# One ring of eight raw slots in the first stage, evenly spread modulation units, and high parts made straight from the slab

## The reference

```python
def ada_params(cond, w, b):
    mod = jax.nn.silu(cond) @ w + b
    return jnp.split(mod, 3, axis=-1)
...
sh_l, sc_l, g_l = ada_params(c, ada_w[layer], ada_b[layer])
sh_c, sc_c, g_c = ada_params(c_ctx, ada_w[layer], ada_b[layer])
xm_l = x_lat * (1.0 + sc_l) + sh_l
xm_c = x_ctx * (1.0 + sc_c) + sh_c
...
mem_n = rmsnorm(mem, norm_mem_w[l])
k = (mem_n @ w_k)
```

## Time and profile before

| | |
|---|---|
| three runs | 3175.62, 3176.96 and 3183.54 us; median 3176.96 us |
| the profiled execution | 3178.01 us |
| its span, first to last instruction | 3176.2 us |
| mean granted TensorE clock | 0.991 of full speed |
| PE busy | 97% of the span |
| DVE busy | 71% |
| ACT busy | 51% |
| data moved | 666.42 MB, mean 210 GB/s |

### The profile page before, as it was taken

How to read it: one execution, slowest core, us unless ns; L and a number is a source line. 1 busy time by engine, 2 the same in 40 slices (tenths; PEclk the granted TensorE clock), 3 DMA queues, 4 the chain that set the end, 5 groups by cost and what they waited for, 6 DMA issues and landing times.

```text
span 3176.2 us, 45015 instructions
## 1 busy us (share of the span) xinstructions
PE 3093.1 (97%) x16842; PEld 2658.5 (84%) x16842; DVE 2244.8 (71%) x2732; ACT 1633.4 (51%) x1984; POOL 59.5 (2%) x52
## 2 busy tenths in 40 slices
PE   7999999999999999999999999999999999999998
PEld 5787877888788887888888888888888888888887
DVE  6779987788768787655767865567457777777544
ACT  6655444555534566544456655445345555555443
POOL 0002300000000000000000000000000000000000
PEclk8999999999999999999999999999999999999999
DMA  7977784787568664655555555566445555555554
GB/s 293 339 256 270 255 296 172 264 311 239 181 211 289 244 220 159 208 182 183 176 186 175 168 189 194 190 225 198 142 146 181 190 189 188 185 185 196 188 191 139
DMA packets 180248, 666.42 MB, mean 210 GB/s; under 512 B 20084, under 2 KB 20468, under 8 KB 178808
## 3 DMA queue, kind: packets, MB, share of 16 engines
q1 hardware_dynamic: 178424, 660.09, 61.2%
q10 hardware_dynamic: 1664, 4.19, 0.3%
HBM read 657.91 MB, written 6.29 MB: 209 GB/s over the span
## 4 chain that ended last, share of the span: by engine, by line
PE 82%; DVE 10%; DMA 3%; ACT 2%; DVEq 1%; issue 1%; ACTq 0%; SPq 0%
PE acc L760 44%; PE acc L764 22%; DVE w_lo L1980 4%; PE acc L771 3%; PE acc L773 3%; PE acc L772 3%; DMA ada_raw<-in_w_ada 1%; ACT w_hi L1275 1%; DVE mod_raw L1991 1%; DMA mod_raw<-in_w_mod 1%; PE acc L928 1%; PE msc L1170 0%; DMA raw<-in_w_mix_out 0%; PE msc L874 0%; PE msc L1190 0%
## 5 line engine op out<-in xcount | busy, mean ns | idle before, releaser
L1980 DVE TENSOR_TENSOR w_lo<-raw,w_hi 128x1024 fp32r<-128x1024 f32 x1020 | 1242.3, 1228 | 561.2 <-ACT w_hi L1275 551.8
L1275 ACT CAST w_hi<-raw 128x1024 fp32r<-128x1024 f32 x1020 | 1061.8, 1049 | 803.2 <-PE acc L764 556.9
L760 PE MATMUL acc<-a_pair,w_hi 128*128 128x512 f32 x2944 | 931.8, 398 | 9.8 <-DVE w_lo L1980 4.1
L764 PEld LDWEIGHTS acc<-a_pair,w_lo 128*128 128x128 f32 x2944 | 554.0, 188 | 131.0
L764 PE MATMUL acc<-a_pair,w_lo 128*128 128x256 f32 x2944 | 579.3, 278 | 0.0
L760 PE MATMUL acc<-b_pair,w_hi 128*128 128x512 f32 x1792 | 571.0, 400 | 5.9 <-DVE w_lo L1980 5.9
L760 PEld LDWEIGHTS acc<-a_pair,w_hi 128*128 128x128 f32 x2944 | 451.2, 189 | 13.4 <-DVE a_pair L2172 3.7
L760 PE MATMUL acc<-f_pair,w_hi 128*128 128x512 f32 x1408 | 442.4, 395 | 0.0
L764 PEld LDWEIGHTS acc<-b_pair,w_lo 128*128 128x128 f32 x1792 | 338.2, 189 | 80.1
L764 PE MATMUL acc<-b_pair,w_lo 128*128 128x256 f32 x1792 | 353.2, 279 | 0.0
L764 PEld LDWEIGHTS acc<-f_pair,w_lo 128*128 128x128 f32 x1408 | 264.5, 188 | 62.5
(11 more groups left out here) (363 smaller groups left out, 2782.6 us busy)
## 6 DMA issues: line engine op xcount, KB each, us to landing
raw<-in_w_ffn_up SPq DMA_DIRECT2D x176, 512.0 KB, 4.1
mod_raw<-in_w_mod SPq DMA_DIRECT2D x128, 512.0 KB, 5.1
raw<-in_w_ffn_down SPq DMA_DIRECT2D x88, 512.0 KB, 3.3
ada_raw<-in_w_ada SPq DMA_DIRECT2D x64, 512.0 KB, 5.7
raw<-in_w_xa_k SPq DMA_DIRECT2D x32, 512.0 KB, 6.5
raw<-in_w_k SPq DMA_DIRECT2D x32, 512.0 KB, 4.7
raw<-in_w_v SPq DMA_DIRECT2D x32, 512.0 KB, 5.0
raw<-in_w_even_out SPq DMA_DIRECT2D x32, 512.0 KB, 4.6
```

The costliest lines, as they stand in the source:

```text
L760: pe.matmul(acc[:, bank(stage, g) + m, :], w_h[:, cols], pair[:, :, kc, :], start=begin, stop=False, skip_group_check=True)
L764: mm = pe.matmul(acc[:, bank(stage, g) + m, 0:T], w_l[:, cols], pair[:, 0, kc, :], start=False, stop=end, skip_group_check=True)
L1275: nc.scalar.copy(w_hi[:, slot], source).then_inc(hi_done, 1)
L1980: vec.tensor_tensor(w_lo[:, slot], source, w_hi[:, slot].bitcast(F32), ALU.subtract).then_inc(lo_done, 1)
```

## The change

It has five parts.

1. **The ring.** In mem_k both kinds use one ring of eight slots, `raw` and `ada_raw` in turn: unit j goes to slot j mod 8 and is fetched when unit j - 8 has been subtracted.
2. **The order of units.** The 58 a behind the first w are spread evenly over 22 w: the runs of three and of two alternate. There are still 14 runs of three and 8 of two, and ten w at the end.
3. **Side work of mem_k.** The high parts of the memory are made at j = 0 (three quarters) and 1, the low parts at j = 0 and 2, squares at 2, 5, 8, 11, sums at 7, 10, 13, 15, root at 16, reciprocal at 17, transposes at 22, their reader at 27. The context is fetched ahead of unit 87 in place of unit 24.
4. **High parts direct.** ACT computes a_hi from `x` itself, two activations (Identity with scale and shift) of 128x256 for one q, in place of one cast of what DVE wrote; DVE makes product and low part of the same q in one step. So q runs at j = 89 to 95 and at unit 0 of ctx_k, and for the latent at j = 9 to 15 of ctx_v and unit 0 of lat_k.
5. **Mods.** ctx_k has two mods (units 13 and 16) in place of five; lat_o has twelve in place of nine.

```diff
@@ Stage
-                take = -(-len(a) // (ADA_OVER - n)) if n < ADA_OVER else 0
-                mixed += [w] + a[:take]
-                a = a[take:]
-            assert not a
+                begin, end = (-(-min(m, ADA_OVER) * len(a) // ADA_OVER) for m in (n, n + 1))
+                mixed += [w] + a[begin:end]
...
-MOD_AT = {"ctx_k": range(8, 18, 2), ...
-          "lat_q": spread(16, 11), "lat_o": spread(16, 9), ...
+MOD_AT = {"ctx_k": (13, 16), ...
+          "lat_q": spread(16, 11), "lat_o": spread(16, 12), ...
...
+CTX_LOAD_AT = 87
+MEM_SQUARE_AT = {2: 0, 5: 1, 8: 2, 11: 3}
+MEM_SUM_AT = {7: 0, 10: 1, 13: 2, 15: 3}
+MEM_ROOT_AT, MEM_SCALE_AT, MEM_TURN_AT, MEM_TAKE_AT = 16, 17, 22, 27
...
+        def first_slot(j):
+            half, slot = divmod(j % (2 * RING), RING)
+            tile, landed = (ada_raw, ada_landed) if half else (raw, raw_landed)
+            return tile[:, slot], landed[slot], 16 * (j // (2 * RING) + 1)
...
@@ load_first, on SP
-                    if j == 24:
-                        sp.wait_ge(pe_step, AFTER["mem_norm"]["pe"])
+                    if j == CTX_LOAD_AT:
+                        sp.wait_ge(pe_step, BEFORE["mem_norm"]["pe"] + 1)
                         nc.sync.dma_start(x[:], t["ctx"]).then_inc(ctx_in, 16)
-                    n = PLACE[kind].index((stage.name, j))
-                    if n >= RING:
-                        sp.wait_ge(lo_done, RING + UNIT_OF[kind][n - RING] + 1)
...
+                    if j >= 2 * RING:
+                        sp.wait_ge(lo_done, j - RING + 1)
+                    slot, landed, _ = first_slot(j)
...
@@ mem_chunks, on ACT
-                if j < 4:
-                    q = j
+                for q in (range(3) if j == 0 else range(3, 4) if j == 1 else ()):
...
-                if j > CTX_AT:
-                    high(j - CTX_AT - 1, 0)
+                if j >= CTX_AT:
+                    if j == CTX_AT:
+                        act.wait_ge(dve_step, AFTER["mod"]["dve"])
+                        act.wait_ge(ctx_in, 16)
+                    high(j - CTX_AT, 0)
...
             def high(q, n):
-                act.wait_ge(chunks_made, 8 * n + q + 1)
-                nc.scalar.copy(a_hi[:, 2 * q:2 * q + 2, :], buf_a[...]).then_inc(chunks_high, 1)
+                which = 1 - n
+                for c in range(2 * q, 2 * q + 2):
+                    mm = nc.scalar.activation(a_hi[:, c, :], x[:, c, :], ACT.Identity, bias=mod[:, c, which:which + 1],
+                                              scale=mod[:, 16 + c, which:which + 1])
+                mm.then_inc(chunks_high, 1)
...
@@ mem_chunks, on DVE
-                if 1 <= j < 5:
-                    q = j - 1
+                for q in (range(3) if j == 0 else range(3, 4) if j == 2 else ()):
...
             def modulated(q, slab, which, n):
-                if 2 <= q < 10:
-                    dve.wait_ge(chunks_high, 8 * n + q - 1)
-                    low(a_hi, a_lo, q - 2)
-                    dve.drain()
-                if q < 8:
-                    for c in range(2 * q, 2 * q + 2):
-                        mm = vec.tensor_scalar(...)
-                    mm.then_inc(chunks_made, 1)
+                for c in range(2 * q, 2 * q + 2):
+                    vec.tensor_scalar(...)
+                dve.drain()
+                dve.wait_ge(chunks_high, 8 * n + q + 1)
+                low(a_hi, a_lo, q)
```

More of the change, by code:

```diff
@@ L191, in ring_place @@
 def ring_place(stage, j):
-    return PLACE["w"].index((stage.name, j)) if stage.ada else stage.u0 + j - ADA_UNITS
+    return stage.u0 + j - STAGES[0].n // 2
 def spread(n, k):
     return [(2 * m + 1) * n // (2 * k) for m in range(k)]
-MOD_AT = {"ctx_k": range(8, 18, 2), "ctx_v": spread(16, 9), "lat_k": spread(18, 13), "lat_v": spread(16, 9),
-          "lat_q": spread(16, 11), "lat_o": spread(16, 9), "pool_u": spread(16, 9), "mlstm_z": spread(16, 13),
+MOD_AT = {"ctx_k": (13, 16), "ctx_v": spread(16, 9), "lat_k": spread(18, 13), "lat_v": spread(16, 9),
+          "lat_q": spread(16, 11), "lat_o": spread(16, 12), "pool_u": spread(16, 9), "mlstm_z": spread(16, 13),
           "pool_z": spread(16, 10), "even_out": range(0, 16, 2), "sgu_u": spread(32, 18), "sgu_z": spread(26, 14)}
@@ L598, in load_first @@
                         load_mem()
-                    if j == 24:
-                        sp.wait_ge(pe_step, AFTER["mem_norm"]["pe"])
+                    if j == CTX_LOAD_AT:
+                        sp.wait_ge(pe_step, BEFORE["mem_norm"]["pe"] + 1)
                         nc.sync.dma_start(x[:], t["ctx"]).then_inc(ctx_in, 16)
-                    n = PLACE[kind].index((stage.name, j))
-                    if n >= RING:
-                        sp.wait_ge(lo_done, RING + UNIT_OF[kind][n - RING] + 1)
[L607 to L612, removed]
+                    if j >= 2 * RING:
+                        sp.wait_ge(lo_done, j - RING + 1)
+                    slot, landed, _ = first_slot(j)
+                    source = t["w_ada"][PLACE["a"].index((stage.name, j))] if kind == "a" else t[stage.weights][stage.group_units * g + k]
+                    nc.sync.dma_start(slot.rearrange("p a b -> p (a b)"), source).then_inc(landed, 16)
             def load(stage):
@@ L804, in mem_sums @@
             def mem_sums(j):
-                q = j - 6
-                if 0 <= q < 4:
+                if j in MEM_SUM_AT:
+                    q = MEM_SUM_AT[j]
                     if q == 0:
@@ L1215, in raw_of @@
             stage, j = unit_at(stage, j)
-            if stage.ada and stage.kinds[j][0] == "a":
-                n = PLACE["a"].index((stage.name, j))
-                return ada_raw[:, n % ADA_RING], ada_landed[n % ADA_RING], 16 * (n // ADA_RING + 1)
+            if stage.ada:
+                return first_slot(j)
             place = ring_place(stage, j)
@@ L1487, in wide_and_last @@
             def wide_and_last(j):
-                if j < 2:
-                    high(6 + j, 0)
+                if j == 0:
+                    high(7, 0)
                 if j == 4:
@@ L1519, in key_tokens @@
                     act.wait_ge(unit_used, RING + STAGE["ctx_v"].u0 + j)
+                    if j == 9:
+                        act.wait_ge(x_in, 16)
                     high(j - 9, 1)
@@ L2322, in ctx_states @@
                     ctx_rows()
[L2323 to L2324 removed]
+                if j >= 9:
+                    if j == 9:
                         dve.wait_ge(x_in, 16)
[L2326 removed]
+                    modulated(j - 9, x, 0, 1)
                 if j == COLUMNS_AT + 1:
```

31 lines of the change are left out of this document (13 added, 18 removed).

## The result

The changed kernel took 3156.79, 3160.03 and 3161.31 us, median 3160.03 us, against 3176.96 us before, three runs each. The ratio is 0.9937, with a 95% interval from 0.9921 to 0.9952: faster by 16.9 us. Run again on another chip its ratio was 0.9934 [0.9921, 0.9948]. The profiled execution took 3160.03 us, with a span of 3158.2 us against 3176.2.

What follows compares the result with a forecast made beforehand. PE was taken as the bound, busy 97% of the span. Gains 2.0 + 13.7 + 3.9 + 2.5 + 0.5 = 22.6 us from 3178.0 gave 3155 us; main case 3147 to 3162, whole range 3146 to 3167.

Steps and rivals of the forecast that it cites:

- Start: mem_k up to 33.49 us: unit 6 and the first sum done at 31.5 us; gain 2.0 us, between 0.5 and 3.5.
- Units 7 to 85: mem_k, 33.49 to 169.17 us: of 19.5 us lost against the dense pace, 13.7 us goes and 5.8 stays.
- store stalls: mem_k: three stalls while ACT waits in store_keys for DVE's scaled keys; 3.5 us of loss expected to stay.
- the slow cycles: mem_k, 65.32 to 130.37 us: ten cycles of one w and three a fall from 6.51 to 5.51 us, 10 us.
- SP's queue and the context: Context fetch moved between units 86 and 87: cost zero while the lead of eight units holds.
- Hand-over: Into ctx_k: PE's 2.20 us wait for the context's last pair goes, with the half-clock matmuls behind it; gain 3.9 us.
- mods in ctx_k: Three mods leave ctx_k, two from ahead of PE's 2.79 us wait for a subtraction; gain 2.5 us, 0 to 2.8.
- Small waits in ctx_v and lat_k: PE's small waits in these two stages: 0.5 us gained, 0 to 2.
- Rival 1: mem_k: the sustained transfer rate, not the lead, stays the limit; 3164 or 3166 us; chance 0.17.
- Rival 2: ACT's direct high parts: Identity alternating with the cast pays table loads, 30 to 41 us added, say 3190; chance 0.04.
- Rival 3: The context arrives late, DVE holds unit 91 back 2.3 us and PE may add 1.7: 3159 us; chance 0.04.
- Rival 4: The gaps only move: w_hi/w_lo slots' cast and subtraction chain sets mem_k's slow cycles; some 6 us gained, 3172; chance 0.10.

Runs made afterwards that it cites:

- ring_only: The kernel before with the ring of eight slots alone, nothing else of the change; 3174.01 us, ratio 0.9979.
- high_old: The changed kernel with the high parts made as before, ACT casting what DVE wrote; 3159.42 us, ratio 0.9941.
- mods_old: The changed kernel with the old places of the mods alone, five in ctx_k and nine in lat_o; 3164.81 us, ratio 0.9957.
- best: mods_moved with three squares, three sums, root and reciprocal of mem_k one or two units earlier; 3154.93 us, ratio 0.9918.
- mods_moved: The changed kernel with lat_k's mods at units 10 to 17 (eight, not thirteen), lat_o 13, pool_u 10, mlstm_z 16; 3155.09 us, ratio 0.9921.
- side_old: The changed kernel with the old places of mem_k's side work alone; 3167.05 us, ratio 0.9965.
- order_old: The changed kernel with the old order of the a units alone; 3156.83 us, ratio 0.9926.

## Why the prediction was right, and where not

The time was 3160.03 us: inside the range of 3146 to 3167, inside the main case's own 3147 to 3162, and 5 us over the 3155 named. Term by term:

- **Start, 2.0 us.** The forecast had unit 6 and the first sum done at 31.5 us; the sum ended at 31.84. Unit 6 began at 25.13, not 24.7, and took 4.98 us, most of it at half clock. Gain 1.65 us. Right.
- **Units 7 to 85, 13.7 us.** 135.68 - 123.81 = 11.9 us. Of the 19.5 us of loss 7.6 stayed, not 5.8. Of these, 4.6 lie from unit 28 on, where I had 3.5 for the store stalls and 1.3 for the other cycles: right, although PE's longest single waits there were only 0.59 and 0.55 us. The other 3.0 us lie ahead of unit 28, where I had 1.0, and 2.43 of them are the wait at unit 21. That is the term that was mis-sized: I charged "1 us for the table load and root on ACT" and let the rest be hidden; on the trace ACT does unit 20 only behind a table load and the root, and on DVE the 1.74 us reciprocal and the 0.69 us epilogue of unit 17 stand ahead of unit 21's subtraction.
- **Where these 11.9 us come from.** I put "10 x (6.51 - 5.51) = 10 us" on the slow cycles; ring_only won 7.2 in them. Undoing the side work cost 7.3 to 7.9 us at ctx_k, with 2.0 for the start in it. That 5.9 + 7.6 = 13.5 is near the 14.3 to 14.9 us at ctx_k is in part luck, since a lead of five cost 12.7. The order and, with eight units queued, the context's place are worth next to nothing. The sum is nearly right; shares that hold in any order it does not have.
- **SP's queue and the context, zero.** Right, closer than I thought, and it hangs on the lead of eight: the context took 10.7 us from issue to landing, and ACT waited 3.05 us for unit 87, but PE went through units 87 to 99 without a pause, 160.62 to 197.12. With five units queued the same fetch cost 6.0 us, the fall of the clock behind it included. Fetched in the slow stretch itself, it cost 0.2 us.
- **Hand-over, 3.9 us, and mods in ctx_k, 2.5 us.** Each was low by about 1 us: 4.8 by high_old, 3.7 by mods_old. ctx_k gave 8.4 us in place of 6.4. This makes up for the middle of mem_k, so that the sum at ctx_v came out as 22.7 against 22.1 by two errors of opposite sign. The three mods put into lat_o cost nothing, as forecast: the lead was 20.2 us at its start and 21.05 at mlstm_z.
- **ACT's price for the direct high parts.** Two activations of 592 ns for a q, as read from L1894's group; covered, as forecast.

```profile
L1464 ACT ACTIVATE a_pair<-x,mod 128x256 fp32r<-128x256 f32 x32 | 17.4, 592 | 4.1 <-DVE kv_stage L2063 4.1
```

- **The step that failed: "The late stages are PE-bound, so the time saved early is kept", with "Small waits in ctx_v and lat_k: 0.5 us gained".** They are not, as far as unit 9 of lat_k. The trace of before showed it: from PE's first matmul of ctx_v to its wait for the gates, the same matmuls as 236.22:308.09 above, DVE was busy for 70.75 of 73.74 us:

```profile
258.50:332.24 73.74, 71.87 (x374) 60.67 (x372) 70.75 (x117) 38.59 (x45) 4.99 (x5) 1.00 0.83 292
```

PE's own waits in it (0.71, 1.15, 0.98 us) looked like single events that a lead would shorten. They were the sign of DVE as the bound. PE now covered the stretch in 71.87 us, 1.9 faster, and then stood 3.32 us in place of 0.98: it gained nothing. From the first unit of ctx_v to the start of the reciprocal of the gates DVE took 76.74 us before and 77.67 after, so its lead of 22.7 us came through to the gates nearly whole, as 21.8. Behind this pause the clock fell, which it had not done there before (in the second execution the granted clock from 312 to 320 us was 0.79). 0.9 us is DVE's; the rest of the 2.4 us between 22.7 and 20.35 goes with the fall. A bound stage did not take the lead away; it kept PE from adding to it, and the long wait cost clock. Behind lat_v the lead rose to 21.4 us at ret_q and then fell by 1.3 in rnn_x (granted clock 0.77 over the 15 us from 1490, before 0.89 over those from 1510), by 0.8 ahead of xa_q, which is open, and by 1.4 in xa_o, a fall of the clock shown below. This is the sign that the forecast had named for being wrong, stages after lat_o that change their length.

**The rivals.** Rival 1 is out: with eight units queued, 13 units in a row landed 1.27 to 1.29 us apart, 512 KB each, which is 410 GB/s, and the first stretch above has 409 GB/s over 20 to 30 us. The section of the Trainium skill's "DMA: Bandwidth & Descriptors" that the prediction drew on, with about 358 GB/s as what binds from HBM, does not hold for this core as it ran here; by that figure a unit would have taken 1.46 us, an estimate, and the measured 1.28 decides. Rival 2: no table load came with the high parts, which took 592 ns each. Rival 3: the context was not late. Rival 4 (the gaps only move): in mem_k no, but its idea came true two stages on.

## What to carry to other kernels

Before you book an early gain to the end, ask at each later stage which engine is busy for nearly all of the stretch between two hand-overs, not which is busiest over the program: behind an engine at 95% there the others gain no more than that engine itself is early, and what they save on the way turns into one longer wait at the end. Movable work (here the mods) belongs where that engine has room, and it is worth measuring a part again once such a place is freed: the direct high parts went from 2.0 to 2.9 us at lat_v to 5.7. Slots for fetched data that are kept apart by kind give the common kind a short lead and the rare kind a long one; one ring over the mixed stream gives every unit the same.

## What the runs showed of the hardware

The start of mem_k ran at two clock levels from execution to execution, with the same instructions in all but one of these kernels (best). In the stretch from 20 to 30 us the granted clock was 0.50 to 0.59 in seven executions with the new side work and a lead of eight, and 0.79 to 0.82 in three (high_old, mods_moved, best). Unit 6 took 4.98 us in the one case and 3.02 in the other:

```profile
20.00:30.00 10.00, 8.85 (x35) 6.44 (x35) 8.57 (x10) 7.12 (x8) 0.00 (x0) 0.82 1.02 408
```

This is mods_moved, beside the first stretch of the changed kernel above. The lead at ctx_k was 13.9 to 14.9 us in the five of the first kind that change nothing in mem_k, and 16.9 and 17.1 us in the two such of the second. It happened late too. Around the 2.36 us wait of xa_o's last pair, with 7.64 us busy in both, the clock fell in the changed kernel and not in mods_moved, and the lead went from 19.4 to 18.0 us in one and stayed in the other. All fourteen executions have this wait of 2.36 us, and in four of them (both of the changed kernel, side_old, order_old) the clock fell behind it. First the changed kernel, then mods_moved:

```profile
2320.00:2330.00 10.00, 7.64 (x34) 6.28 (x34) 2.40 (x4) 2.55 (x3) 0.00 (x0) 0.83 0.17 52
```

```profile
2310.00:2320.00 10.00, 7.64 (x41) 6.37 (x40) 3.82 (x4) 2.55 (x3) 0.00 (x0) 1.00 0.19 64
```

So differences of 2 to 3 us between single profiles of this kernel are within what such falls make; the ratios of five rounds, or the same gap in several traces, are what a claim of that size needs. Why a pause brings the clock down in one execution and not in another is open.
